# Routing weights moved into the experts' hidden rows, and expert outputs added to the residual by accumulating gathers

## What is computed

```python
def hier_moe(xn, ...):                    # T = 1280 tokens, D = 1024, 32 experts
    g_idx = argmax(xt @ w_rg + b_rg)      # one of 4 groups
    top_v, top_i = top_k(el_sel, 2)       # two of the 8 experts in that group
    ew = softmax(top_v) * g_w             # the two routing weights of a token
    ...
    def expert_block(xb, eb):             # D_EXPERT = 512
        hb = silu(xb @ w_gate[eb]) * (xb @ w_up[eb])
        return hb @ w_down[eb]
    y = segment_sum(yrows[dest] * swt[:, None], stok)

x = x + out_projection(...)               # pooling mixer and mLSTM ahead of it
xn2 = rmsnorm(x, norm2_g)
x = x + hier_moe(xn2, ...)
return rmsnorm(x, final_norm_g)
```

## Time and profile before

| | |
|---|---|
| median of 3 runs | 1238.58 us (1236.71 to 1238.65) |
| the profiled execution | 1236.62 us, its span 1234.9 us |
| PE busy | 1113.7 us, 90% of the span |
| DVE busy | 866.8 us, 70% |
| ACT busy | 684.6 us, 55% |
| POOL busy | 185.3 us, 15% |
| DMA | 324.04 MB, mean 262 GB/s |

### The profile page before, as it was taken

One profiled execution on the slowest core, in us unless ns is written; L12 is line 12 of the kernel. 1 busy time (PEld: TensorE's weight loads), 2 busy tenths in 40 slices (PEclk: granted clock), 3 DMA queues, 4 the chain that ended last, 5 costly groups with the idle time before them and its releaser, 6 DMA issues.

```text
span 1234.9 us, 17854 instructions
## 1 busy us (share of the span) xinstructions
PE 1113.7 (90%) x5679; PEld 935.0 (76%) x5679; DVE 866.8 (70%) x1340; ACT 684.6 (55%) x1128; POOL 185.3 (15%) x285
## 2 busy tenths in 40 slices
PE   5999999998998999992899999999999999999910
PEld 4888888887888788881688888888888888888710
DVE  5649510234447656665688999999999999999958
ACT  5432241233346544213677877877787787787623
POOL 1100210011100012223011211221221221121100
PEclk9999999999999899995899999999999999999965
DMA  8212240455979344446789999999999999999667
GB/s 236 59 29 83 86 129 1 142 175 199 318 265 334 130 139 151 163 154 228 269 313 374 372 377 385 378 380 391 382 380 394 382 378 391 383 372 387 241 251 298
DMA packets 135808, 324.04 MB, mean 262 GB/s; under 512 B 23552, under 2 KB 60320, under 8 KB 135760
## 3 DMA queue, kind: packets, MB, share of 16 engines
q1 hardware_dynamic: 119856, 281.80, 63.1%
q0 software_dynamic: 15904, 41.61, 8.7%
HBM read 285.35 MB, written 51.11 MB: 272 GB/s over the span
## 4 chain that ended last, share of the span: by engine, by line
PE 78%; DVE 9%; ACT 6%; DMA 3%; issue 3%; POOL 0%; ACTq 0%; SPq 0%; POOLq 0%; DVEq 0%
PE psum L808 23%; PE psum L810 22%; PE psum L809 22%; DVE e_lo L1723 3%; ACT e_hi L1284 3%; PE psum L1024 2%; PE psum L979 1%; PE psum L1057 1%; ACT h_fb L1241 1%; DVE x L1834 1%; DVE x L1842 1%; PE psum L922 1%; DVE x L1832 1%; PE psum L863 1%; PE psum L967 1%
## 5 line engine op out<-in xcount | busy, mean ns | idle before, releaser
L1723 DVE TENSOR_TENSOR e_lo<-e_st,e_hi 128x1024 fp32r<-128x1024 f32 x384 | 442.6, 1219 | 15.6 <-ACT e_hi L1284 14.4
L1284 ACT ACTIVATE e_hi<-e_st 128x1024 fp32r<-128x1024 f32 x384 | 372.3, 1053 | 9.4 <-PE psum L810 8.4
L808 PE MATMUL psum<-e_hi,ex_hi 128*128 128x512 f32 x512 | 203.8, 398 | 8.6 <-DVE ex_lo L1765 3.7
L810 PE MATMUL psum<-e_hi,ex_lo 128*128 128x512 f32 x512 | 200.8, 392 | 0.0
L809 PE MATMUL psum<-e_lo,ex_hi 128*128 128x512 f32 x512 | 200.3, 391 | 0.0
L808 PE MATMUL psum<-xT_hi,w_hi 128*128 128x512 f32 (+1 forms) x408 | 147.1, 361 | 4.5 <-DVE xT_lo L1403 3.0
L809 PE MATMUL psum<-xT_lo,w_hi 128*128 128x512 f32 (+1 forms) x408 | 145.4, 356 | 0.0
L810 PE MATMUL psum<-xT_hi,w_lo 128*128 128x512 f32 (+1 forms) x408 | 145.3, 356 | 0.0
L808 PEld LDWEIGHTS psum<-e_hi,ex_hi 128*128 128x128 f32 x512 | 96.6, 189 | 41.4 <-DVE e_lo L1723 16.3
L810 PEld LDWEIGHTS psum<-e_hi,ex_lo 128*128 128x128 f32 x512 | 96.5, 189 | 20.8
L809 PEld LDWEIGHTS psum<-e_lo,ex_hi 128*128 128x128 f32 x512 | 96.6, 189 | 19.3
(11 more groups left out here) (234 smaller groups left out, 1722.3 us busy)
## 6 DMA issues: line engine op xcount, KB each, us to landing
e_st<-in_expert_w_gate_dram SPq DMA_DIRECT2D x128, 512.0 KB, 4.7
e_st<-in_expert_w_up_dram SPq DMA_DIRECT2D x128, 512.0 KB, 7.3
e_st<-in_expert_w_down_dram SPq DMA_DIRECT2D x128, 512.0 KB, 8.6
mlstm_units<-stage SPq DMA_DIRECT2D x18, 640.0 KB, 3.8
w_st<-in_w_in_dram SPq DMA_DIRECT2D x20, 512.0 KB, 4.1
xn_scratch<-xn POOLq DMA_DIRECT2D x20, 512.0 KB
f_y<-expert_rows SPq DMA_DIRECT2D x20, 512.0 KB, 12.1
stage<-gate_rows SPq DMA_DIRECT2D x18, 512.0 KB, 6.0
```

The lines of the kernel that those rows point to most:

```text
L808: pe.matmul(out, a_hi, b_hi, start=start, stop=False)
L810: return pe.matmul(out, a_lo, b_hi, start=False, stop=stop)
L1284: act.activation(e_hi[:, r, :, :], e_st[:, slot, :, :], ACT.Copy).then_inc(ehi_done, 1)
L1723: dve.tensor_tensor(e_lo[:, r, :, :], e_st[:, slot, :, :], e_hi[:, r, :, :].bitcast(F32), ALU.subtract).then_inc(elo_done, 1)
```

## The change

1. The routing weights leave the end of the program. `wts` is turned by one PE transpose, copied to `w_rows` and stored in DRAM (`w_dram`, in the order of the entries). In each step POOL gathers the 128 weights of the expert's rows (`weights_in`, one 4-byte element for each row) into a column of `w_row`, and the product that makes `hh` multiplies by it. The expert's output rows are then already weighted.
2. `final_sum` and the loads of `f_y` go. POOL adds the rows to the residual tiles by indirect gathers with `compute_op=ALU.add` (`add_rows`): first entries of 10 tiles, second entries of 10 tiles, both from `y_dram`, and then 10 gathers from `last_dram`, which holds the rows of the last expert; SP stores these from `yo`. A tile's gather waits until the one before it on the same pair of tiles has landed (`rows_added`, a semaphore for two tiles).
3. For this, VectorE computes two tables of row numbers between the second and the third expert step (`entry_tables`, 19 small instructions): `rest_rows` (entries that lie in the last expert point past the table and are skipped) and `last_rows`. POOL sends the rows of the expert before the last to the last expert's places of `y_dram` as well.
4. Semaphores are shared to make room. The load of an mLSTM unit 4 to 7 waits for the load that used its semaphore before. The final gain and the squares' scratch go into slots of `e_st`.

```diff
+            def weights_in(i, b):
+                rows = rows_to[:, i:i + 1] if isinstance(i, int) else row_of[:, b:b + 1]
+                pool.indirect_dma_start(
+                    out=w_row[:, b:b + 1], out_offset=None, in_=w_dram,
+                    in_offset=bass.IndirectOffsetOnAxis(ap=rows, axis=0),
+                    bounds_check=2 * T - 1, oob_is_err=False).then_inc(factor_in[b], 16)
+
+            def add_rows(i, rows, earlier, table):
+                if earlier:
+                    pool.wait_ge(rows_added[i // 2], 32 * earlier)
+                pool.indirect_dma_start(
+                    out=x1[:, order[i], :], out_offset=None, in_=table,
+                    in_offset=bass.IndirectOffsetOnAxis(ap=rows, axis=0), compute_op=ALU.add,
+                    bounds_check=table.shape[0] - 1, oob_is_err=False).then_inc(rows_added[i // 2], 16)
...
+            weights_in(0, 0)
+            weights_in(1, 1)
...
             with pool.Fori(2, n_half) as j:
                 rows_in(2 * j + 1, 1)
                 rows_out(2 * j - 2, 0)
+                weights_in(2 * j + 1, 1)
                 rows_in(2 * j + 2, 0)
                 rows_out(2 * j - 1, 1)
+                weights_in(2 * j + 2, 0)
             rows_out(2 * n_half - 2, 0)
-            rows_out(2 * n_half - 1, 1)
...
+            pool.indirect_dma_start(
+                out=y_dram, out_offset=bass.IndirectOffsetOnAxis(ap=row_to[:, 1:2], axis=0),
+                in_=yo[:, 0, :], in_offset=None, bounds_check=2 * T - 1, oob_is_err=False).then_inc(y_out[0], 16)
+            pool.wait_ge(weights_step, 4)
+            pool.wait_ge(y_out[0], 16 * n_half + 16)
...
+            for k in range(2):
+                for i in range(NT):
+                    add_rows(i, rest_rows[:, i, k:k + 1], k, y_dram)
+            pool.wait_ge(last_out, 16)
+            for i in range(NT):
+                add_rows(i, last_rows[:, i:i + 1], 2, last_dram)
...
-            def hidden(i):
+            def hidden(i, b):
                 dve.wait_ge(sg_done, i + 1)
+                dve.wait_ge(factor_in[b], slot_loads(i, b))
                 wait(dve, ht_ready, i)
-                dve.tensor_tensor(hh[:, :], psum[:, 1, :], sg[:, :], ALU.mult).then_inc(h_ready, 1)
+                dve.scalar_tensor_tensor(out=hh[:, :], in0=psum[:, 1, :], scalar=w_row[:, b:b + 1], in1=sg[:, :],
+                                         op0=ALU.mult, op1=ALU.mult).then_inc(h_ready, 1)
...
             step(1, 1, split=4)
+            entry_tables()
             step(2, 0)
...
-            for b in range(2):
-                sp.wait_ge(y_out[b], 16 * n_half)
...
-            for t in range(NT):
-                for k in range(2):
-                    sp.dma_start(f_y[:, t, k, :], y_dram[k * T + t * P:k * T + (t + 1) * P, :]).then_inc(tile_in[t], 16)
...
+            sp.wait_ge(y_left, last + 1)
+            sp.wait_ge(y_right, last + 1)
+            sp.dma_start(last_dram[:, :], yo[:, 1, :]).then_inc(last_out, 16)
...
             for t in range(NT):
-                act.wait_ge(f_sum, t + 1)
+                act.wait_ge(rows_added[t // 2], 96)
...
-            def final_sum(t):
-                dve.wait_ge(tile_in[t], 32 + units_signalled(t))
-                link(dve.scalar_tensor_tensor(out=x1[:, t, :], in0=f_y[:, t, 0, :], scalar=wts[:, 0, t:t + 1],
-                                              in1=x1[:, t, :], op0=ALU.mult, op1=ALU.add))
-                dve.scalar_tensor_tensor(out=x1[:, t, :], in0=f_y[:, t, 1, :], scalar=wts[:, 1, t:t + 1],
-                                         in1=x1[:, t, :], op0=ALU.mult, op1=ALU.add).then_inc(f_sum, 1)
```

More of the change, by code:

```diff
@@ L215, in build @@
     assert m_off[0] <= END - 4 * NT * D
[L217 to L219 removed]
+    w_rows = at("w_rows", ROWS, [2 * NT, P], F32)
+    w_row = at("w_row", ROWS + KB, [P, 2], F32)
+    slot_e = at("slot_e", ROWS + KB + 64, [P, NT, 2], I32)
+    in_last = at("in_last", ROWS + KB + 192, [P, NT, 2], F32)
+    last_key = at("last_key", ROWS + KB + 320, [P, NT, 2], F32)
+    last_min = at("last_min", ROWS + KB + 448, [P, NT], F32)
+    rest_rows = at("rest_rows", ROWS + KB + 512, [P, NT, 2], I32)
+    last_rows = at("last_rows", ROWS + KB + 640, [P, NT], I32)
     psum = nc.alloc_psum_tensor("psum", [P, 8, 512], F32)
@@ L258, in build @@
         masked, kq_ready, wgt_done, s_done = (sem(n) for n in ("masked", "kq_ready", "wgt_done", "s_done"))
-        tile_in = [sem(f"tile_in{i}") for i in range(NT)]
+        unit_in = [sem(f"unit_in{i}") for i in range(4)]
+        rows_added = [sem(f"rows_added{i}") for i in range(NT // 2)]
         num_ready, kv_ready, rdn_done, state_done, h_done = (
@@ L289, in build @@
         y_out = [sem(f"y_out{i}") for i in range(2)]
-        f_out, gf_in, f_sum, f_root, f_done = sem("f_out"), sem("gf_in"), sem("f_sum"), sem("f_root"), sem("f_done")
+        f_out, f_root, f_done = sem("f_out"), sem("f_root"), sem("f_done")
+        weights_step, last_out = sem("weights_step"), sem("last_out")
+        factor_in = [sem(f"factor_in{i}") for i in range(2)]
         pool_past = sem("pool_past")
@@ L1065, in _ @@
             ex_transposes(0, 0)
+            pe.wait_ge(weights_step, 1)
+            pe.transpose(psum[0:2 * NT, 7, 0:P], wts[:, 0:2, :].rearrange("p k t -> p (k t)"),
+                         ident[:, :]).then_inc(weights_step, 1)
             gate_up(0, 0)
@@ L1757, in _, with weights_out, entry_tables @@
             link(dve.reciprocal(wts[:, 0, :], wts[:, 2, :]))
-            link(dve.tensor_tensor(wts[:, 1, :], wts[:, 0, :], rd21[:, :], ALU.mult))
+            dve.tensor_tensor(wts[:, 1, :], wts[:, 0, :], rd21[:, :], ALU.mult).then_inc(weights_step, 1)
+            link(dve.memset(w_row[:, :], 0.0))
+            def weights_out():
+                dve.wait_ge(weights_step, 2)
+                dve.tensor_copy(w_rows[:, :], psum[0:2 * NT, 7, 0:P]).then_inc(weights_step, 1)
+            def entry_tables():
+                first_slot = rt[:, 331:332]
+                dve.tensor_scalar(first_slot, half_steps[:, 2:3], float(E * P), None, ALU.mult)
+                link(dve.tensor_scalar(slot_e[:, :, :], slot_i[:, :, :], E - 1, None, ALU.bitwise_and))
+                link(dve.tensor_scalar(last_key[:, :, :], slot_e[:, :, :], float(E - 1), None, ALU.is_equal))
+                link(dve.scalar_tensor_tensor(out=in_last[:, :, :], in0=slot_i[:, :, :], scalar=first_slot,
+                                              in1=last_key[:, :, :], op0=ALU.is_ge, op1=ALU.mult))
+                for i in range(NT):
+                    entries = rowval[:, :, order[i]]
+                    dve.scalar_tensor_tensor(out=rest_rows[:, i, :], in0=in_last[:, i, :], scalar=2.0 * T, in1=entries,
+                                             op0=ALU.mult, op1=ALU.add)
+                link(dve.tensor_scalar(last_key[:, :, :], slot_i[:, :, :], first_slot, float(E - 1), ALU.subtract,
+                                       ALU.subtract))
+                link(dve.tensor_scalar(last_key[:, :, :], last_key[:, :, :], 1.0 / E, -2.0 * T, ALU.mult, ALU.add))
+                link(dve.tensor_tensor(last_key[:, :, :], last_key[:, :, :], in_last[:, :, :], ALU.mult))
+                link(dve.tensor_reduce(last_min[:, :], last_key[:, :, :], AX.X, ALU.min))
+                dve.tensor_scalar(last_rows[:, :], last_min[:, :], 2.0 * T, None, ALU.add).then_inc(weights_step, 1)
             def ex_lo_part(i, b):
@@ L1795, in step @@
                     lo_part(down_piece(i, c))
-                hidden(i)
+                hidden(i, b)
                 ex_lo_part(i + 1, 1 - b)
@@ L1811, in _ @@
                 lo_part(gu_piece(1, c))
-            hidden(0)
+            hidden(0, 0)
             ex_lo_part(1, 1)
@@ L1840, in final_norm @@
                 if t == 0:
-                    dve.wait_ge(gf_in, 16)
-                dve.scalar_tensor_tensor(out=x1[:, t, :], in0=x1[:, t, :], scalar=wts[:, 3, t:t + 1],
-                                         in1=gf_b[:, :], op0=ALU.mult, op1=ALU.mult).then_inc(f_done, 1)
-            for t in range(NT + 1):
-                if t < NT:
-                    final_sum(t)
-                if t >= 1:
-                    final_norm(t - 1)
+                    dve.wait_ge(norms_in, 48)
+                x1_t = x1[:, order[t], :]
+                dve.scalar_tensor_tensor(out=x1_t, in0=x1_t, scalar=wts[:, 3, t:t + 1],
+                                         in1=e_st[:, gu_piece(0, 0)[1], :, :].rearrange("p a n -> p (a n)"),
+                                         op0=ALU.mult, op1=ALU.mult).then_inc(f_done, 1)
+            for t in range(NT):
+                final_norm(t)
 _INS = ["x_prompt", "x_sample", "norm1_g", "w_in", "pool_w", "pool_scale", "gate_b", "head_norm_g", "w_out",
```

68 lines of the change are left out of this document (43 added, 25 removed).

## The result

The changed kernel takes 1266.87 us (median of 4 runs, 1261.95 to 1268.48); the kernel before took 1238.62 beside it. The ratio is 1.0222, with an interval of 1.0189 to 1.0255: slower by 28 us, where 15.5 were forecast, and outside the range of 1234 to 1262. A second set of runs of the same kernel gave 1263.33 us and 1.0194 [1.0164, 1.0224]. The profiled execution took 1261.95 with a span of 1260.2, 25.3 more than the span of 1234.9 before. It is the fastest of the four, 4.9 us under their median, where the profiled execution before is 2.0 under its own; so some 3 of the 28 us lie in no profile.

A forecast was written before the change was run, and what follows sets the result against it. TensorE bounds the steps, VectorE's chain and full DMA engines the end. Gathers from 1182.55, first pair 1229.25, ScalarE to 1245.85, end 1250.4: 15.5 us over span 1234.9, so 1238.58 + 15.5 = 1254.1 us; range 1234 to 1262.

The forecast's parts named there:

- the transfer's 44 us: At the end, moving 10.16 MB by adding gathers: 44 us, between 36.3 (three movements for two) and 48.4 (twice the work).
- dearer still: Rival for the end: each adding gather holds POOL or the DMA 2.57 us; 1263.9 us or more, chance 0.12.
- Weights in the steps, 0: In the expert steps, gathering the weights and multiplying them into `hh` costs 0 us.
- The tables, 2.15 us: Behind the second expert, `entry_tables` on VectorE makes TensorE 2.15 us late (0 to 3.8), never given back.
- Start of the gathers, 1182.55: At the end, the adding gathers begin at 1182.55: second scatter landed at 1180.4, plus 2.15 for the tables.
- Issue, 1.28 us each: At the end, 20 gathers in one POOL queue start 1.28 us apart (0.97 and a gap of 0.30).
- faster: Rival for the end: copy price and issues running ahead of the data, transfer 24.2 us; 1234.3 us, chance 0.15.
- the rival of copy price: Rival for the end: additions cost what a copy costs, POOL's issue is the bound; 1237.2 us, chance 0.15.
- between: Rival for the end: 31 to 36 us of transfer, a slowdown of 2.5 to 7.8 us; chance 0.06.
- ScalarE's run of 16.6, then 4.55: Behind the gathers, ScalarE takes 16.6 us for ten tiles; last reciprocal and norm 1.5 and store 3.05 follow.
- the break-even: At the end, the transfer time at which the change neither wins nor loses: 28.5 us, or 1.43 us per gather.

The follow-up runs named there:

- tables_early: The changed kernel with `entry_tables` called ahead of the first expert's `ex_lo` instead of behind the second expert; 1260.68 us, ratio 1.0177 to the kernel before.
- no_rows: The changed kernel with the row-number bound of the 30 adding gathers set to 0, so all rows but number 0 are skipped; 1255.96 us (one run).
- one_pass: The changed kernel without the 10 gathers of the second choice's rows, so 20 adding gathers in place of 30; 1241.34 us (one run).
- plain_gathers: The changed kernel with the add taken out of the 30 gathers at the end, which then overwrite the residual tiles; 1239.65 us, ratio 1.0009.

## Why the prediction was wrong in size

The direction and the mechanism were right: an end that waits for adding gathers and then runs at ScalarE's pace. The step that failed is the third of the list for the end, **the transfer's 44 us**, and with it the chance that I gave to "dearer still". Against the median the forecast misses by 12.8 us, 1266.87 where it had 1254.1. 9.8 us of it show in the spans and are taken apart here; the other 3 are the distance of the median from the profiled execution, and no profile has them. By its own steps:

- *Weights in the steps, 0*: right to 0.4 us. TensorE works 99.31 of 100 us, and in the waits of 660 to 1150 us nobody waits for `w_row`. In a steady step its gather takes POOL 1.97 us, not 1.15, and POOL's idle time covers that.
- *The tables, 2.15 us*: right, 2.1 by TensorE's wait and by tables_early. The last `yo` copy came 3.7 us later than in the profile before. The other 1.5 us are there already at the first `hh`, which started at 605.37 where it was 603.80; a third of them ahead of `ex_lo` (589.29, before 588.75), the rest where the granted clock of 592 to 600 us was 0.50 and 0.89, and before 0.74 and 1.00. That is inside the difference between two executions, and its cause is open.

```profile
605.37 0.75 DVE L1867 SCALAR_TENSOR_TENSOR hh<-psum,w_row,sg 128x512 f32<-128x512 f32 x1 [0.98 <-ACT sg L1392]
```

- *Start of the gathers, 1182.55*: measured 1184.99. Of the 2.4 us, 1.5 are those just named. The other 0.9 are POOL's own start. The second scatter was issued at 1180.80, where the sum had it but for those 1.5 us, and I let the first gather begin 3.3 us behind that; it began 4.19 behind: the scatter had landed after 3.31 us, and the gather started 0.88 behind the landing. POOL's indirect transfers start as late behind the copy of `row_to` (0.88), which I had counted there and not here.
- *Issue, 1.28 us each*: measured 1.87 (1.57 and 0.30). The trace before had only plain indirect transfers, and I carried their price over to adding ones without a margin. Nothing in the sum rested on it, since the transfer was taken as longer still, but the rival "faster" and the rival of copy price did: at 1.87, 20 issues are 37 us, and no transfer, however quick, would have saved the change (no_rows, one execution, but 17 us over the kernel before). The case "between", too, could not come.
- *Transfer, 44 us (36.3 or 48.4)*: the first pair was complete 53.8 us behind the first gather where the sum had 46.7. The rate is that of the upper bound, twice a copy's work: 211 GB/s against 420 at a full DMA share. For 10.16 MB this makes 48.2 us, and 46.6 by the 2.33 us per gather of one_pass. The row pointed there, a share of 1.03 with nothing idle; I shaded it to 44 by the argument that the write side doesn't double, for which no row spoke. So of the 7.1 us the transfer's rate has 2.6 to 4.2, and the rest, 2.9 to 4.5 us, lies outside it: the sum had 2.7 for issue and landing, where 5.6 to 7.2 us were left. The uneven first slices (71 to 208 GB/s) and the store of the last expert's rows lie in the same stretch; neither was tried alone, and how the 7.1 us divide stays open inside these bounds.
- *ScalarE's run of 16.6, then 4.55*: right, 16.85 and 4.55.

The misses add up: 1.5 + 0.9 + 7.1 + 0.25 = 9.8 us, and 15.5 + 9.8 = 25.3, the difference of the two spans.

"Collectives: The Full Stack", the page of the Trainium skill that the prediction cites, section "The bandwidth ceiling: the fold count and why AG ≠ RS ≠ AR", states that an add in the DMA path runs at half a copy's rate, because it reads two sources. This case's trace agrees closely: 211 against 420 GB/s in loads and 393 in plain gathers. Its figure in GB/s for one engine does not carry over: the estimate from it was 41 us for these rows, and the runs have 46.6 to 48.2.

The rival "dearer still" (0.12) put the first pair at 1239.05 and the span's end at 1260.2, and that is where they came, 1238.79 and 1260.2. That the numbers meet so closely is partly luck: the rival starts at 1182.55 and has 56.5 us to the first pair, and the kernel started 2.4 us later and needed 53.8. It had named two ways to get there: POOL held for 2.57 us, which is wrong (1.87), or the DMA engines for that long, which is nearly right (2.33 to 2.41). The rival of copy price holds for copies: it had 1237.2 us, and plain_gathers has 1239.65. But I had tied the break-even to the transfer's time alone, and by no_rows it needs the shorter issue as well.

## What to carry to other kernels

By these runs an addition in a transfer is paid twice, with half the rate on the DMA engines and with more than half again as long an issue on GpSimd; it can win only where both the transfer engines and GpSimd have idle time, and the work that it takes off an engine was the bound; no run here found such a place. Here the DMA engines were full nearly wherever the additions could stand, at the end up to about 1220 us, and in the steps too. When the trace of before has full transfer engines, price a second read as twice the work, and price the issue of a new form of instruction with a margin of its own, since it can decide even where the bytes are free.

## What the hardware showed that I had not expected

- The issue of an adding gather takes GpSimd 1.57 us whether rows land or not (no_rows: 1.57 with 1 GB/s moved), that of a plain one 0.99 (plain_gathers).
- An addition on GpSimd (128x1024, 2.34 us) and VectorE's additions hold each other up: 3.36 us for 1.22.
- The gather of 128 weights, one word each, takes GpSimd 1.97 us right behind a scatter, and that of 128 rows of 4 KB behind a copy 1.15; the one of 1.92 in the earlier trace rows stands behind another indirect transfer too. In these rows the issue with the fewer bytes takes longer.
- Executions with the same instructions reach the last expert's end up to 4.7 us apart (1179.32 and 1183.98). 2.1 us of it go with a lower granted clock in the first steps, the rest is ahead of them, and what causes either is open; it is why the tails and not the spans are compared above.
